# Expert weights of a two-block transformer: one transfer a tile with 8 KB runs, in place of two with 4 KB

## The reference

```python
def grouped_moe(x, router_w, router_bias, w_gate, w_up, w_down):
    scores = jax.nn.softmax((xt @ router_w).astype(jnp.float32), axis=-1)
    ...
    for e in range(N_EXPERTS):                               # 16
        he = jax.nn.silu(xt @ w_gate[e]) * (xt @ w_up[e])    # 256 x 1024 @ 1024 x 512
        y = y + combine[:, e:e + 1] * (he @ w_down[e]).astype(jnp.float32)   # @ 512 x 1024
```

## Time and profile before

| | before |
|---|---|
| time, median of 3 runs | 2187.9 us (2186.85 to 2191.44) |
| profiled execution, span | 2187.5 us |
| PE busy | 1962.1 us, 90% |
| PE weight loads (PEld) busy | 1488.9 us, 68% |
| DVE, ACT, POOL busy | 746.8, 737.2, 1008.6 us |
| moved by DMA | 477.02 MB |

### The profile page before, as it was taken

How to read it: one execution, slowest core, us unless ns; L and a number is a source line. 1 busy time by engine, 2 the same in 40 slices (tenths; PEclk the granted TensorE clock), 3 DMA queues, 4 the chain that set the end, 5 groups by cost and what they waited for, 6 DMA issues and landing times. The chain is left out here.

```text
span 2187.5 us, 29236 instructions
## 1 busy us (share of the span) xinstructions
PE 1962.1 (90%) x11525; PEld 1488.9 (68%) x11525; DVE 746.8 (34%) x1336; ACT 737.2 (34%) x1026; POOL 1008.6 (46%) x784
## 2 busy tenths in 40 slices
PE   7879888999789997999887898999999997887998
PEld 5556654555367774554476686789988997767997
DVE  3453232111433133111244777821163214533112
ACT  3332320011233231111134545544364444444342
POOL 6326500000345630000174284088888886516886
PEclk9979998999899998999997998999999999998999
DMA  7535668999857649999953153056565665304662
GB/s 260 191 115 199 235 253 340 409 409 409 301 205 251 237 169 382 409 409 409 367 167 116 58 184 96 1 155 190 181 181 174 181 190 169 116 10 135 183 185 95
DMA packets 294981, 477.02 MB, mean 218 GB/s; under 512 B 16762, under 2 KB 196973, under 8 KB 294733
## 3 DMA queue, kind: packets, MB, share of 16 engines
q1 hardware_dynamic: 288812, 459.82, 59.5%
q10 hardware_dynamic: 6048, 15.53, 2.0%
HBM read 474.15 MB, written 1.15 MB: 217 GB/s over the span
## 5 line engine op out<-in xcount | busy, mean ns | idle before, releaser
L644 POOL TENSOR_TENSOR w_lo<-raw,w_hi 128x512 fp32r<-128x512 f32 x780 | 1008.4, 1327 | 1162.4 <-ACT w_hi L1426 1162.4
L710 PE MATMUL PS<-at_hi,w_hi 128*128 128x256 f32 x1680 | 488.4, 291 | 20.8 <-DVE at_lo L1935 16.9
L1426 ACT ACTIVATE w_hi<-raw 128x2048 fp32r<-128x2048 f32 x195 | 371.7, 1908 | 344.2 <-PE PS L712 335.8
L711 PE MATMUL PS<-at_lo,w_hi 128*128 128x256 f32 x1680 | 481.2, 286 | 0.0
L712 PE MATMUL PS<-at_hi,w_lo 128*128 128x256 f32 x1680 | 481.1, 286 | 0.0
L710 PEld LDWEIGHTS PS<-at_hi,w_hi 128*128 128x128 f32 x1680 | 328.7, 196 | 35.4 <-DVE at_lo L1935 16.3
L711 PEld LDWEIGHTS PS<-at_lo,w_hi 128*128 128x128 f32 x1680 | 328.7, 196 | 3.7 <-issue 2.6
L712 PEld LDWEIGHTS PS<-at_hi,w_lo 128*128 128x128 f32 x1680 | 328.3, 195 | 0.0
L710 PE MATMUL PS<-w_hi,at_hi 128*128 128x512 f32 (+1 forms) x480 | 192.6, 401 | 31.3 <-DVE at_lo L1935 13.7
L711 PE MATMUL PS<-w_lo,at_hi 128*128 128x512 f32 (+1 forms) x480 | 187.8, 391 | 0.0
L712 PE MATMUL PS<-w_hi,at_lo 128*128 128x512 f32 (+1 forms) x480 | 187.6, 391 | 0.0
(11 more groups left out here) (312 smaller groups left out, 2499.9 us busy)
## 6 DMA issues: line engine op xcount, KB each, us to landing
raw<-ffn_w_gu SPq DMA_DIRECT2D x132, 512.0 KB, 5.0
raw<-ada_w SPq DMA_DIRECT2D x64, 768.0 KB, 5.3
raw<-ffn_w_down SPq DMA_DIRECT2D x66, 512.0 KB, 4.1
raw<-l_e_up SPq DMA_DIRECT2D x48, 512.0 KB, 15.1
raw<-diff_w_in SPq DMA_DIRECT2D x48, 512.0 KB, 4.6
raw<-l_xkv SPq DMA_DIRECT2D x32, 512.0 KB, 5.6
w_plain_hi<-l_e_gate SPq DMA_DIRECT2D x32, 512.0 KB, 15.0
w_plain_lo<-l_e_gate SPq DMA_DIRECT2D x32, 512.0 KB, 15.3
```

The source lines that it names most:

```text
L644: ins = nc.gpsimd.tensor_tensor(w_lo[:, n % RING, part], raw[:, order_of(n) % RAW, part], w_hi[:, n % RING, part].bitcast(F32), ALU.subtract)
L710: pe.matmul(dst, s_hi, m_hi, start=first, stop=False)
L711: pe.matmul(dst, s_hi, m_lo, start=False, stop=False)
L1426: nc.scalar.activation(w_hi[:, n % RING, :], raw[:, s % RAW, :], ACT.Copy).then_inc(hi_done, 1)
```

## The change

A tile is one DMA of 1 MiB. Partition q of a gate or up tile holds the four rows 4q to 4q + 3 of its 512, partition q of a down tile the rows 2q and 2q + 1 of its 256. Either way it is one run of 8 KB, in HBM as in SBUF. PE waits for 16 on `moe_landed` in place of 32. The columns of X in the gather's stationary operand are now four apart (`i=4`), 16 bytes, where they were two apart. The columns of `hid` in a transpose are two apart (`hid_cols`), 8 bytes, where they were adjacent. Which inputs and hidden values come together in one matmul changes with it, and so does the order of the sums.

```diff
-        Xk = X[:, :, :].rearrange("p t (c q i) -> p t c i q", c=4, i=2)
+        Xk = X[:, :, :].rearrange("p t (c q i) -> p t c i q", c=2, i=4)
+
+        hid_cols = hid.rearrange("p (c q i) -> p c i q", c=2, i=2)
...
-                    t = moe_slot(at, layer)
-                    for j in range(2):
-                        sp.dma_start(t[:, j * D:(j + 1) * D], rows[j]).then_inc(moe_landed[slot], 16)
+                    sp.dma_start(moe_slot(at, layer), rows).then_inc(moe_landed[slot], 16)
                     at += 1
...
-                            load_expert([w[e, (2 * h + j) * 256:(2 * h + j + 1) * 256, :].rearrange("(q i) n -> q (i n)", i=2)
-                                         for j in range(2)])
+                            load_expert(w[e, h * 512:(h + 1) * 512, :].rearrange("(q i) n -> q (i n)", i=4))
...
-                            load_expert([dw[e, (2 * h + j) * P:(2 * h + j + 1) * P, :] for j in range(2)])
+                            load_expert(dw[e, h * 256:(h + 1) * 256, :].rearrange("(q i) n -> q (i n)", i=2))
...
-                    pe.wait_ge(moe_landed[slot], 32 * (layer * in_layer + m // MOE_RING + 1))
+                    pe.wait_ge(moe_landed[slot], 16 * (layer * in_layer + m // MOE_RING + 1))
...
-                            ins = pe.matmul(PS[:, 6 + k // 4, (k % 4) * P:(k % 4 + 1) * P], Xk[:, t, k // 2, k % 2, :],
+                            ins = pe.matmul(PS[:, 6 + k // 4, (k % 4) * P:(k % 4 + 1) * P], Xk[:, t, k // 4, k % 4, :],
                                             onehot_t[:, t, :], start=t == 0, stop=t == NT - 1)
...
-                        ins = pe.transpose(PS[:, 5, j * P:(j + 1) * P], hid[:, j * P:(j + 1) * P], ident[:, :])
+                        ins = pe.transpose(PS[:, 5, j * P:(j + 1) * P], hid_cols[:, j // 2, j % 2, :], ident[:, :])
```

More of the change, by code:

```diff
@@ L1220, in experts_all @@
                         for i in range(2):
-                            ins = pe.transpose(PS[:, 4 + j, (2 * i + t) * P:(2 * i + t + 1) * P], Xk[:, t, j, i, :], ident[:, :])
+                            ins = pe.transpose(PS[:, 4 + j, (2 * i + t) * P:(2 * i + t + 1) * P], Xk[:, t, (2 * j + i) // 4, (2 * j + i) % 4, :], ident[:, :])
                 ins.then_inc(g["x_full"], 1)
@@ L1261, in experts_all @@
                             for t in range(NT):
-                                at = (2 * e + t) * 512 + j * P
+                                h = all_h[:, (2 * e + t) * 512:(2 * e + t + 1) * 512].rearrange("p (c q i) -> p c i q", c=2, i=2)
                                 ins = pe.transpose(PS[:, 4 + 2 * e + j // 2, ((j % 2) * NT + t) * P:((j % 2) * NT + t + 1) * P],
-                                                   all_h[:, at:at + P], ident[:, :])
+                                                   h[:, j // 2, j % 2, :], ident[:, :])
                     ins.then_inc(g["ht_full"], 1)
```

## The result

Four timed runs of the changed kernel have a median of 2233.9 us (2229.1 to 2237.4), four of the kernel before 2187.4 us (2186.9 to 2191.4). The ratio is **1.0204, 95% interval 1.0186 to 1.0221**: 2% slower (the two medians divided give 1.0212, inside the interval). The forecast was 2234 us. The profiled execution has a span of 2235.6 us against 2187.5, 48.1 us more.

What follows compares the result with a forecast made beforehand. The prediction took PE to end last in the expert layers, just behind saturated transfers. From 2187.5 us, less 5.2 for tile waits, plus 51.2 for the gather, it got 2233.5, forecast 2234 us, range 2182 to 2252.

Steps and rivals of the forecast that it cites:

- What bounds the kernel: Expert layers: PE and transfers both full, PE ends last; faster expert transfers can give only 5.2 us.
- -5.2 us for the waits: Expert layers: PE's waits for expert tiles, 5.2 us over both layers, go with faster transfers.
- Rate of 8 KB runs: Expert tile transfers: between 409 GB/s (no gain) and 424 GB/s, with 424 taken as the value.
- The gather's step: PE's gather matmuls: 16 byte column step takes the time from record to record from 121 ns up by 105 ns.
- 480 records at the full clock, 32 at half: Gather on PE: 480 records add 50.4 us, 32 in first gathers add 0.8 us, together +51.2 us.
- Sum: Whole kernel: 2187.5 - 5.2 + 51.2 = 2233.5 us, forecast as 2234.
- The transposes of `hid`: PE's 64 transposes, columns now 8 bytes apart: load needs 5 ns more, 0.3 us in all, counted as nothing.
- the free step: Rival, gather: 16 byte step costs PE nothing and the kernel gets faster, 2182.3 us; chance 0.15.
- the small price: Rival, gather: each new line costs a little, 7.7 us less 5.2, giving 2190 us; chance 0.10.
- the half-hidden load: Rival, gather: load partly hidden behind the matmul, step 150 to 190 ns, about 2207 us; chance 0.08.
- The clock: Rival, expert layers: PE's clock falls in the slower gathers, losing 43 us, 2277 us; chance 0.05.
- The runs were not cut: Rival, expert transfers: 8 KB runs are cut into 4 KB, changing only whether the 5.2 us go; no chance given.

Runs made afterwards that it cites:

- e2: The kernel before, with two transfers of 4 KB runs a tile, but the gather reads columns of X 16 bytes apart: 2240.9 us, ratio 1.0233.
- e6: The changed kernel, one transfer of 8 KB runs a tile, but the gather reads columns of X 8 bytes apart: 2183.1 us, 0.9962 of the kernel before.
- e5: The kernel before, with 4 KB runs, but the gather reads adjacent columns of X in place of every second: 2189.8 us, ratio 0.9995.
- e1: The kernel before, with each expert tile in one DMA of 1 MiB, still in runs of 4 KB; PE's reads unchanged: 2187.6 us, ratio 0.9993.

## Why the prediction was right, point by point

- **What bounds the kernel**: right. PE ended last and the transfers gave only PE's waits for tiles. e2 shows that a slower gather comes out in the layers in full, e6 that faster transfers give the waits alone. For the kernel before, "PE ends last" says a little too much: e5 took 2.8 us from the gathers and the waits grew by 3.5, so PE and the transfers nearly tie there.
- **-5.2 us for the waits**: they went. Freed of the gather's price (e6) the layers fell by 7.8 us, of which 1.7 are the clock in the first gathers; with the 0.6 us that the transposes cost, the waits were worth about 6.7. The term was 1.5 us too small, since it counted PE's idle time alone.
- **Rate of 8 KB runs**: 424 GB/s taken, 421 in the full slices of e6 and 421 to 429 after. The pick at the high end was right.
- **The gather's step**: 105 ns more forecast, 236.5 - 121 = 115 measured. The price of a place was taken as 1.75 ns: the load at 8 bytes, less a fixed part of 84 ns that comes from loads of adjacent columns, over 64 places. The three points give 2.08 ns a place and leave a fixed part of 329 - 128 x 2.08 = 63, so 308 ns were forecast for the load and 329 came. For the step the forecast took 128 x 1.75 = 224 ns, with the fixed part left out as hidden, and the measured rise in the step is 1.8 ns a place. That the 1.75 came so near to this, and to DVE's 1.77, is in part luck: it rests on the wrong fixed part, and the reduces compared in the earlier trace rows also differ in their form (four sums against one).
- **480 records at the full clock, 32 at half**: a miscount. A layer has one first gather, 32 records, so there are 64 of those and 448 others. 448 x 115.2 ns = 51.6 us, and 2 x (7.73 - 6.76) = 1.9 us for the first ones, 53.5 against the 51.2 of the sum. The first gather grew by 31 ns a record where 25 was forecast.
- **Sum**: 53.5 + 0.6 - 6.7 = 47.4 us by the measured terms, against 47.3 in the windows and 46.0 forecast. The errors in step, count and waits nearly cancelled: with the right count and its own step the forecast would have been 2187.5 - 5.2 + 448 x 0.105 + 1.6 = 2230.9, also within its range. So the mechanism was right, and that 2234 met 2233.9 to a tenth is luck; four runs of the changed kernel differ by 8 us among themselves.
- **The transposes of `hid`**: counted at nothing, 0.04 us each group of four, 16 x 0.04 = 0.6 us. Their load rose from 140 to 205 ns, far more than the 5 ns of the forecast, but most of it lies beside the matmul.
- **The rivals**: the free step, the small price and the half-hidden load all fall with 329 ns. The clock stayed at 0.99 over the layers. The runs were not cut: the page has 27,650 packets fewer, which are, but for 2, 24,576 of data and 192 x 16 = 3,072 more, 16 for each DMA that disappeared. e1, where the same DMAs disappeared and the runs stayed 4 KB, has 3,074 fewer.

## What to carry to other kernels

A layout that makes a transfer's runs longer can make an engine's reads sparser, and the two sides must be priced together: here 12 GB/s more were worth 7 us, and the reads cost 54. Count the separate places of 16 bytes that a stationary operand lies in; with fewer than two float32 from each, the weight load here grew by 2.1 ns a place and the step between records by 1.8. Where a sparse operand is read many times (here 8 pairs read X in full), let an idle engine bring it into order once, and keep the transfers.

## What was not expected of the hardware

- **The price of a place is not tied to TensorE's clock.** In the changed kernel's window from 874.5 to 878.0 us, inside the first gather of layer 1, the granted clock is 0.50, that is 1.2 GHz, and yet the group takes 7.73 us as all others do, and no load of the 512 is over 330 ns:

```profile
874.50:878.00 3.50, 3.50 (x15) 3.50 (x16) 0.00 (x0) 0.00 (x0) 0.00 (x0) 0.50 1.02 424
```

With the columns 8 bytes apart the first gather took 6.76 us and the others 4.04, so there the clock did count. The loads of that first gather, in the kernel before from 341 to 348 us:

```profile
L1120 PEld LDWEIGHTS PS<-PB,X x32: 196/331/336, 340.9 to 347.3; 128*128 128x128 f32 x32
```

At the lower clock a load at 8 bytes takes 331 ns, as long as one at 16 bytes takes at either. So the price of the lower clock and that of the places do not add; why is open.

- **A load that rose by half and cost little.** The transposes of `hid`, with adjacent columns, in the kernel before:

```profile
L1165 PEld LDWEIGHTS PS<-ident,PB x64: 138/140/143, 367.9 to 1073.2; 128*128 128x128 f32 x64
```

They load 128 adjacent columns in 140 ns, where the gather takes 192 for as many, and at a step of 8 bytes 205 ns, where the gather takes 196. A group of four grew by 0.04 us only. Why the two differ when adjacent is open; no run was made on it.
